# Down-projections of the second block with 7 block products in place of 8 for 1024 of 2816 features

## The reference

```python
def swiglu_2(h, w_gate, w_up, w_down):
    return (jax.nn.silu(h @ w_gate) * (h @ w_up)) @ w_down
...
        x = x + 0.5 * swiglu_2(rms_norm_2(x, ffn1_norm[l]), ffn1_w_gate[l], ffn1_w_up[l], ffn1_w_down[l])
```

## Time and profile before

| | |
|---|---|
| median of 3 runs | 1736.2 us |
| profiled execution | 1736.38 us, of which span 1734.6 us |
| TensorE busy | 1726.9 us (100%), 10296 matmuls |
| VectorE busy | 1230.0 us (71%) |
| ScalarE busy | 989.6 us (57%) |
| GpSimd busy | 111.4 us (6%) |
| HBM read | 312.10 MB, 181 GB/s over the span |

### The profile page before, as it was taken

How to read it: one execution, slowest core, us unless ns; L and a number is a source line. 1 busy time by engine, 2 the same in 40 slices (tenths; PEclk the granted TensorE clock), 3 DMA queues, 4 the chain that set the end, 5 groups by cost and what they waited for, 6 DMA issues and landing times.

```text
span 1734.6 us, 25928 instructions
## 1 busy us (share of the span) xinstructions
PE 1726.9 (100%) x10296; PEld 1487.0 (86%) x10296; DVE 1230.0 (71%) x1904; ACT 989.6 (57%) x1591; POOL 111.4 (6%) x196
## 2 busy tenths in 40 slices
PE   9999999999999999999999999999999999999999
PEld 7888888888888888888888888888888888888887
DVE  5877765668886777467756887775587648878762
ACT  6766554645555755365545666554565447666551
POOL 2100000702210000000001010000000001000000
PEclk9999999999999999999999999999999999999999
DMA  8545564654343555545454345555355534336551
GB/s 328 190 160 209 188 219 165 226 177 163 146 159 125 191 189 218 192 165 189 184 210 148 124 146 200 196 189 217 145 204 188 216 126 175 143 145 219 193 219 73
DMA packets 45561, 314.82 MB, mean 181 GB/s; under 512 B 5072, under 2 KB 5584, under 8 KB 8448
## 3 DMA queue, kind: packets, MB, share of 16 engines
q1 hardware_dynamic: 45056, 312.54, 49.2%
q10 hardware_dynamic: 288, 0.52, 0.1%
q0 software_dynamic: 96, 0.10, 0.0%
HBM read 312.10 MB, written 1.05 MB: 181 GB/s over the span
## 4 chain that ended last, share of the span: by engine, by line
PE 95%; DVE 1%; ACT 1%; DMA 1%; issue 1%; POOL 0%; SPq 0%; POOLq 0%; DVEq 0%; ACTq 0%
PE P L451 93%; DMA raw<-w_all 1%; PE P L464 1%; PE P L767 1%; DVE wl L1867 1%; ACT wh L1298 1%; PE P L668 0%; ACT nV L1338 0%; PE P L1202 0%; ACT xx L1333 0%; ACT wh L1311 0%; PE P L473 0%; PE P L1121 0%; PE P L1067 0%; DVE fce L2350 0%
## 5 line engine op out<-in xcount | busy, mean ns | idle before, releaser
L1867 DVE TENSOR_TENSOR wl<-raw,wh 128x2048 fp32r<-128x2048 f32 x287 | 656.5, 2294 | 184.5 <-ACT wh L1298 161.8
L1298 ACT ACTIVATE wh<-raw 128x2048 fp32r<-128x2048 f32 (+1 forms) x290 | 550.2, 1901 | 192.0 <-PE P L451 172.3
L451 PE MATMUL P<-xx,wh 128*128 128x512 f32 (+2 forms) x2800 | 643.1, 384 | 0.0
L451 PEld LDWEIGHTS P<-xx,wh 128*128 128x128 f32 (+1 forms) x2800 | 505.4, 188 | 96.7
L451 PE MATMUL P<-xx,wl 128*128 128x256 f32 x2688 | 350.8, 284 | 0.1
L451 PEld LDWEIGHTS P<-xx,wl 128*128 128x128 f32 x2688 | 340.3, 191 | 10.7 <-issue 0.3
L1434 ACT ACTIVATE ft<-P 128x256 f32<-128x256 f32 x240 | 90.1, 382 | 231.5 <-PE P L451 231.5
L451 PE MATMUL P<-wh,fhh 128*128 128x512 f32 x528 | 206.2, 390 | 0.0
L451 PE MATMUL P<-wh,fhl 128*128 128x512 f32 x528 | 205.5, 389 | 0.0
L451 PE MATMUL P<-wl,fhh 128*128 128x512 f32 x528 | 205.5, 389 | 0.0
L2030 DVE TENSOR_TENSOR fg<-P,ft 128x256 f32<-128x256 f32 x240 | 101.7, 424 | 121.9 <-ACT ft L1434 116.6
(11 more groups left out here) (340 smaller groups left out, 1458.7 us busy)
## 6 DMA issues: line engine op xcount, KB each, us to landing
raw<-w_all SPq DMA_DIRECT2D x289, 1024.0 KB, 4.8
nB<-rpb SPq DMA_DIRECT2D x4, 512.0 KB, 7.6
raw<-w_all SPq DMA_DIRECT2D x2, 512.0 KB, 7.0
xs<-x_in SPq DMA_DIRECT2D x1, 1024.0 KB, 9.4
fgb<-post SPq DMA_DIRECT2D x2, 512.0 KB, 5.6
out<-xs SPq DMA_DIRECT2D x4, 256.0 KB, 2.0
C<-cst SPq DMA_DIRECT2D x1, 770.5 KB, 8.7
ntm<-x_in ACTq DMA_DIRECT2D x2, 256.0 KB, 5.2
```

The costliest lines, as they stand in the source:

```text
L451: return t_.on.matmul(o, l, r, start=start, stop=stop, skip_group_check=True)
L1298: a.on.activation(o, i, ACT.Copy).then_inc(*hi.up((m,)))
L1867: v.on.tensor_tensor(o, i, h.bitcast(F32), ALU.subtract).then_inc(*lo.up(m))
```

## The change

In stages 4, 6, 7 and 9, eight of the 22 feature blocks are taken in pairs ("couples" (4,5), (6,7), (8,9), (10,11)). For such a pair, two tiles of tokens and two halves of outputs form a 2x2 by 2x2 product of blocks, done by seven block products and sums of blocks (Winograd's form of Strassen's scheme) in place of eight block products. Each block product is still three matmuls. The down pieces are ordered P S P S P S P S P P P: D1, D3, D5, D7 are the S pieces, each with both halves of one pair (21 matmuls); the other fourteen feature blocks are in the seven P pieces (24 matmuls).

- In the gate/up phase VectorE forms four sums of hidden features per pair (`couple_sums`), ScalarE rounds them (`couple_high`), VectorE takes the rest (`couple_low`).
- In the down-projection VectorE forms four sums T of weight blocks from the raw tile of each S piece (`sums_first`, at p = 0, 2, 4, 6), ScalarE rounds them (`sums_high`), VectorE takes the rest (`sums_low`). They lie in `xx`, one set for all four pairs, so that a set waits for TensorE's end with the one before. High and low parts of an S piece itself have 1536 columns.
- SP overwrites the raw tile of an S piece only when T has been formed from it (`"read"`).
- Products M1, M5, M6, M7 gather in banks 0, 1, 6, 7 over all four pairs, the others in banks 2, 3, 4 (bank 5 has no pair product). At p = 8 VectorE puts them together and into the residual (`sevens_end`), and adds the first half there, which was done at p = 5.
- The first turns of the next stage stand in D9 in place of D6.

Some buffers are laid out anew over existing memory, and the host packs the S pieces. The core of the diff:

```diff
+SEVEN = "PSPSPSPSPPP"
+COUPLES = [(4, 5), (6, 7), (8, 9), (10, 11)]
+SUMS_AT = {0: 0, 2: 1, 4: 2, 6: 3}
+SUMS_IN = (0, 0, 0, 0)
+SINGLE = [k for k in range(NF) if all(k not in c for c in COUPLES)]
+ALONE = [(k, h) for h in range(2) for k in SINGLE]
+LASTS = max(p for p in range(11) if SEVEN[p] == "S")
+MBANK = {"M1": 0, "M5": 1, "M6": 6, "M7": 7}
...
+    def sevens(name, layer):
+        left, couples = list(ALONE), list(COUPLES)
+        for kind in SEVEN:
+            if kind == "P":
+                out.append(("H", name, layer, tuple(left[:4])))
+                del left[:4]
+            else:
+                out.append(("S", name, layer, couples.pop(0)[0]))
...
+        SUM = tuple((h_[:, 0, :], h_[:, 1, :], f_[:, 1, :]) for h_, f_ in ((x2, xf2), (AF["fT"], AF["fTf"])))
+        SEVENS = [BASE[s_] + NF + p for s_ in (4, 6, 7, 9) for p in range(11) if SEVEN[p] == "S"]
...
+        def before_sums(s, u):
+            back = [w for w in range(u) if SUMS_IN[w] == SUMS_IN[u]]
+            if back:
+                return [mm.of("sum", s, back[-1])]
+            return [af.of("hh", s, NF - 1)] if SUMS_IN[u] else [mm.of("piece", BASE[s] + NF - 1)]
...
                     q.wait_ge(*lo.of(m - RAW))
+                    if m - RAW in SEVENS:
+                        q.wait_ge(*ls.of("read", m - RAW))
...
+                cbank = {(0, 0): 2, (1, 0): 3, (0, 1): 4, (1, 1): 5}
...
+                def three(b, ah_, al_, bh, bl, ready, end):
+                    if b not in begun:
+                        claim(b)
+                    t_.wait_ge(*ready[0])
+                    mul(P[b][:, :], ah_, bh, b not in begun, False)
+                    t_.wait_ge(*ready[1])
+                    mul(P[b][:, :], ah_, bl, False, False)
+                    t_.wait_ge(*ready[2])
+                    begun.add(b)
+                    return mul(P[b][:, :], al_, bh, False, end)
...
+                    B21, B11, B22 = (slice(a, a + 512) for a in (0, 512, 1024))
+                    T1, T3, T2, T4 = (slice(a, a + 512) for a in (0, 512, 1024, 1536))
...
+                    of_x(MBANK["M1"], k, 0, wh[n][:, B11], wl[n][:, B11], lo.of(m + p), whole)
+                    e = of_x(2, k + 1, 0, wh[n][:, B21], wl[n][:, B21], lo.of(m + p), ends[0, 0] == p)
+                    if ends[0, 0] == p:
+                        e.then_inc(*mm.up(("half", s, 0, 0)))
+                    of_s(4, 3, wh[n][:, B22], wl[n][:, B22], lo.of(m + p), False).then_inc(*mm.up(("piece", m + p)))
+                    t_.wait_ge(*hs.of("T", s, u, 0))
+                    of_s(MBANK["M5"], 0, th_[:, T1], tl_[:, T1], ls.of("T", s, u, 0), whole)
+                    of_s(MBANK["M7"], 1, th_[:, T3], tl_[:, T3], ls.of("T", s, u, 0), whole)
+                    t_.wait_ge(*hs.of("T", s, u, 1))
+                    of_s(MBANK["M6"], 2, th_[:, T2], tl_[:, T2], ls.of("T", s, u, 1), whole)
+                    e = of_x(3, k + 1, 1, th_[:, T4], tl_[:, T4], ls.of("T", s, u, 1), ends[1, 0] == p)
+                    e.then_inc(*mm.up(("sum", s, u), *([("half", s, 0, 1)] if ends[1, 0] == p else [])))
...
+                def after_seven(p, i, t):
+                    if s < 9:
+                        if p == 9 and i == 1:
                             turn(s + 1, 0, 0)
                             turn(s + 1, 1, 0)
-                        if t == 1 and i == 41:
+                        if t == 1 and p == 10 and i == 1:
                             turn(s + 1, 0, 1)
...
+                if m in SEVENS:
+                    w = 1536
...
+                def couple_high(u):
+                    a.wait_ge(*ls.of("S0", s, u))
+                    a.on.activation(flat(AF["fS"][:, u, 0, :, :]), flat(AF["fSf"][:, u, 1, :, :]),
+                                    ACT.Copy).then_inc(*hs.up(("S", s, u)))
+                def sums_high(u):
+                    h_, l_, f_ = sums(u)
+                    for z in range(2):
+                        n = slice(z * 1024, z * 1024 + 1024)
+                        a.wait_ge(*ls.of("T0", s, u, z))
+                        a.on.activation(h_[:, n], f_[:, n], ACT.Copy).then_inc(*hs.up(("T", s, u, z)))
...
+                    if s not in POST and p in SUMS_AT:
+                        sums_high(SUMS_AT[p])
+                    if s not in POST and p == 9 and s < 9:
...
+                def couple_sums(u):
+                    k = COUPLES[u][0]
+                    A1, A2 = fh[:, k % 3, :], fh[:, (k + 1) % 3, :]
+                    S1, S3, S2, S4 = (AF["fSf"][:, u, 1, i, :] for i in range(4))
+                    v.wait_ge(*vf.of("h", s, k + 1))
+                    v.on.tensor_tensor(S1, A1[:, toks(1)], A2[:, toks(1)], ALU.add).then_inc(*ls.up(("S1", s, u)))
+                    v.on.tensor_tensor(S3, A1[:, toks(1)], A1[:, toks(0)], ALU.subtract).then_inc(*ls.up(("S3", s, u)))
+                    v.wait_ge(*ls.of("S1", s, u))
+                    v.on.tensor_tensor(S2, S1, A1[:, toks(0)], ALU.subtract).then_inc(*ls.up(("S2", s, u)))
+                    v.wait_ge(*ls.of("S2", s, u))
+                    v.on.tensor_tensor(S4, A2[:, toks(0)], S2, ALU.subtract).then_inc(*ls.up(("S0", s, u)))
...
+                def couple_low(u):
+                    h_, l_ = (flat(AF["fS"][:, u, i, :, :]) for i in range(2))
+                    v.wait_ge(*hs.of("S", s, u))
+                    v.on.tensor_tensor(l_, flat(AF["fSf"][:, u, 1, :, :]), h_.bitcast(F32), ALU.subtract).then_inc(*ls.up(("S", s, u)))
...
+                def sums_first(u):
+                    n = m + NF + [p for p in range(11) if SEVEN[p] == "S"][u]
+                    h_, l_, f_ = sums(u)
+                    r_ = raw[n % RAW]
+                    v.wait_ge(*hi.of(n))
+                    for signal_ in before_sums(s, u):
+                        v.wait_ge(*signal_)
+                    v.on.tensor_tensor(grp(f_[:, 0:1024], 2), r_[:, 1536:2048].unsqueeze(1).broadcast_to([128, 2, 512]),
+                                       grp(r_[:, 512:1536], 2), ALU.subtract).then_inc(*ls.up(("T0", s, u, 0)))
+                    v.wait_ge(*ls.of("T0", s, u, 0))
+                    v.on.tensor_tensor(f_[:, 1024:1536], r_[:, 512:1024], f_[:, 512:1024],
+                                       ALU.subtract).then_inc(*ls.up(("T2", s, u)))
+                    v.wait_ge(*ls.of("T2", s, u))
+                    v.on.tensor_tensor(f_[:, 1536:2048], r_[:, 0:512], f_[:, 1024:1536],
+                                       ALU.subtract).then_inc(*ls.up(("T0", s, u, 1), ("read", n)))
+                def sums_low(u):
+                    h_, l_, f_ = sums(u)
+                    for z in range(2):
+                        n = slice(z * 1024, z * 1024 + 1024)
+                        v.wait_ge(*hs.of("T", s, u, z))
+                        v.on.tensor_tensor(l_[:, n], f_[:, n], h_[:, n].bitcast(F32),
+                                           ALU.subtract).then_inc(*ls.up(("T", s, u, z)))
+                def gather(t, hf, src):
+                    return v.on.scalar_tensor_tensor(xs[:, t, halfs(hf)], src, rh_[:, t:t + 1], xs[:, t, halfs(hf)], ALU.mult, ALU.add)
+                def sevens_end():
+                    banks = (2, 3, 4, 5)
+                    M1, M5, M6, M7 = (P[MBANK[n]][:, :] for n in ("M1", "M5", "M6", "M7"))
+                    U2, U3 = AF["ftm"][:, 0, 0:512], AF["ftm"][:, 0, 512:1024]
+                    M1s = AF["ftm"][:, 1, 0:512]
+                    v.wait_ge(*gx.of("rh", s))
+                    v.wait_ge(*mm.of("sum", s, len(COUPLES) - 1))
+                    v.on.tensor_copy(M1s, M1).then_inc(*ls.up(("M1", s)))
+                    v.wait_ge(*ls.of("M1", s))
+                    v.on.tensor_tensor(U2, M6, M1s, ALU.add).then_inc(*ls.up(("M6", s)))
+                    v.wait_ge(*ls.of("M6", s))
+                    v.on.tensor_tensor(U3, M7, U2, ALU.add).then_inc(*ls.up(("M7", s)))
+                    gather(0, 0, M1s).then_inc(*ls.up(("x00", s)))
+                    v.wait_ge(*ls.of("M7", s))
+                    gather(1, 0, U3).then_inc(*ls.up(("x10", s)))
+                    v.wait_ge(*ls.of("x00", s))
+                    add(s, 0, 0, banks, 0.5)
+                    v.wait_ge(*ls.of("x10", s))
+                    add(s, 0, 1, banks, 0.5)
+                    gather(1, 1, U3).then_inc(*ls.up(("x11a", s)))
+                    v.on.tensor_tensor(U2, M5, U2, ALU.add).then_inc(*ls.up(("U4", s)))
+                    v.wait_ge(*ls.of("x11a", s))
+                    gather(1, 1, M5).then_inc(*ls.up(("x11", s), ("M5", s)))
+                    v.wait_ge(*ls.of("U4", s))
+                    gather(0, 1, U2).then_inc(*ls.up(("x01", s)))
+                    v.wait_ge(*ls.of("x01", s))
...
                 rest(NF - 1)
                 banks = (2, 3, 4, 5)
                 for p in range(11):
+                    if s not in POST and p in SUMS_AT:
+                        sums_first(SUMS_AT[p])
+                    if s not in POST and p == LASTS + 1:
+                        sevens_end()
```

(40 more changed lines are left out.)

55 lines of the change are left out of this document (53 added, 2 removed).

## The result

| | median | range | against before, 95% interval |
|---|---|---|---|
| before | 1736.14 us | 1735.94 to 1736.23 | |
| after | 1761.61 us | 1761.05 to 1762.16 | 1.0144 [1.0132, 1.0156] |

The change makes the kernel 25.5 us slower; the forecast was 1760.7 us, 24.5 slower. One execution of the kernel before, run beside the last experiment, took 7890.72 us and is left out of all comparisons. From the profile page of the changed kernel, the lines that answer to the earlier trace rows: busy time by engine, and the lines of the chain that ended last.

The account below looks back on a forecast made before the run. TensorE, busy for all but 8 us, was taken to bound the kernel. Stages 6 and 7 at +6.5 us each, stage 4 at +6.9 and stage 9 at +4.5 were summed to +24.5 on 1736.2: 1760.7 us, range 1748 to 1772.

Parts of the forecast that it names:

- The signs: Down-projections: high parts idle for DMA, T sums 11.7 to 11.9 us apart, four TensorE waits a stage of 1.5 to 2.2.
- One sign of being wrong: Listed against the forecast: T sums 10.2 us apart, TensorE waits in the gate/up phase, or a granted clock below 1.00.
- The gain: TensorE in the four down-projections: 48 matmuls removed at 0.2267 us, 10.9 us, all on the path.
- The pair sums at nothing: Gate/up phase: sums of hidden features, 1.7 us a pair on VectorE, hidden beside TensorE and costed at nothing.
- The cover of 2.6 us a pair: Gate/up phase: VectorE's spare time beside TensorE, 1.3 us a piece, claimed to hide the pair sums.
- The ramp: Start of each down-projection: T's first low part stands at 9.74 us, TensorE wants it at 7.71 and waits 2.0.
- the added 0.36: Stage 4: VectorE leaves the gate/up phase 0.36 us later than in stage 6, lengthening the first wait.
- The turn: Down-projection loop from one T through fetch, high and low part to the next T: 11.75 us against TensorE's 10.20.
- the landing: Time for D4's fetch into D1's raw tile to arrive, within the loop between two T: 4.8 us.
- The fetch: Weight fetch of 1024 KB: 4.4 us by the skill page, median 4.8 in the trace; the page's total 6 us smaller.
- The tail: End of stages 4, 6, 7: TensorE waits 2.0 us for the addition before the third turn of `xs`; none in 9.
- The clock rival: TensorE: about 19 new gaps each drop the clock to 1.2 GHz for 11 matmuls, 47 us, some 1808; chance 0.03.

Follow-up runs that it names:

- the last experiment: Changed kernel with the fetches of D4, D6, D8, D10 and of the piece right behind each cut to half their bytes: 1746.78 us.
- opened through the tile: Changed kernel with D4, D6, D8, D10 fetched into memory free in the down-projection, computing instructions and order unchanged (also called the four tiles aside): 1737.02 us.
- opened through the order: Changed kernel with the low parts of D4, D6, D8 moved on VectorE behind the next T (also called VectorE's order alone): 1745.78 us.
- T's low part first: Changed kernel with T's low part made ahead of the other piece's low part in VectorE's order: 1760.44 us.
- the kernel that has no gap in the four stages: Changed kernel with VectorE's order rewritten and, on ScalarE, T's roundings ahead of the next high part; nothing left out: 1725.80 us.

## Why the prediction was right

- **The signs.** ScalarE's high parts of D4, D6, D8 and D10 do idle for the DMA, the T sums stand 11.5 to 11.9 us apart, and the third turn waits in stages 4, 6 and 7 and not in 9. Of the four waits a stage on T's low part, 13 of 16 came: in stages 6, 7 and 9 the second is missing (below). One sign of being wrong came too, a mean granted clock below 1.00 (0.997).
- **The gain**, 48 matmuls at 0.2267 us, 10.9: measured alone 10.7.
- **The pair sums at nothing**: confirmed by leaving them out. Each small addition was under-priced. From the groups by form of after, stages 5 and 6:

```profile
L2194 DVE TENSOR_TENSOR fSf<-fh,fSf 128x128 f32<-128x128 f32 x4 | 1.2, 293 | 0.1
L2208 DVE TENSOR_TENSOR xf<-raw 128x1024 f32<-128x1024 f32 x4 | 4.9, 1218 | 0.0
```

  0.29 us and not half of 0.42, since half the columns don't halve the operation. The cover of 2.6 us a pair was wide enough. The broadcast form of T, priced from rows of other operations at 1.22, came to 1.218; the 1536-column part, priced at 1.75 from a line between two sizes, to 1.75.
- **The ramp**: M5's second matmul went 9.96 us behind D0's start, not 9.74, because VectorE came out at 4.43 and not 4.2. I had dated D0 from its end, back over 24 matmuls; the first start lay 0.25 us earlier. The wait is 2.2 us, not 2.0. In stage 4 VectorE came out at the same 4.4, and the added 0.36 was not there.
- **The turn**: 11.5 to 11.9 us against 11.75, the landing 4.6 to 5.0. The second matmul of M5 went 9.96, 21.68, 33.18 and 45.47 us behind D0's start in stage 4. The prediction's times for it, without the 0.36 that it added for this stage, are 9.74, 21.49, 33.24 and 45.53. Four experiments move the turn and the time goes with it: opened through the tile (1737.0), opened through the order (1745.8), shortened by 0.3 and 0.9 us (1755.5, 1746.8). Two that leave it alone, though they take away a wait or a cost next to it, move little (1760.4, 1760.6).
- **The fetch.** The chain has landings of 4.6 to 5.0 us, with a second fetch behind, and halving both brought the landing to 3.85. The Trainium skill, "DMA: Bandwidth & Descriptors", Anatomy of one DMA, gives by its formula for the software path an estimated 4.4 us for 1024 KB and 3.2 for 512 KB. Both are below what this case's trace has on SP's queue, and with 4.4 the forecast would have been 6 us lower.
- **The tail**: TensorE's third turn started 1.65, 1.74 and 1.90 us late against 2.0, and moving one low part removed it.
- **The sum of the lag**: 35.0 us against 35.2 forecast (four times 7.2, the tails and stage 4's 0.36). That it is this close is in part luck. VectorE's exit was dated 0.23 us too early in four stages (+0.9 us), the turn 0.07 too long fifteen times (-1.0) and stage 4's 0.36 didn't come. The forecast's four stages also add up to 24.4 us, not 24.5.
- **The clock rival**, at 0.03, was half right, and "the rows at hand show no fall" was too weak a ground. One of the two rows was misread. The 2.75 us of idleness at the start lie ahead of TensorE's first instruction, and the first matmuls ran slow. TensorE's timeline of the kernel before:

```profile
2.75 2.08 PE L451 MATMUL P<-C 128*128 128x128 f32 x8 [2.75 <-DMA C<-cst]
4.61 1.06 PE L464 MATMUL P<-C,ntm 128*128 128x128 f32 x4
5.47 2.13 PE L451 MATMUL P<-C 128*128 128x128 f32 x12
...
13.02 1.03 PE L464 MATMUL P<-C,ntm 128*128 128x128 f32 x8
13.81 1.17 PE L451 MATMUL P<-wl,xx 128*128 128x512 f32 x4
```

  The four of L464 at 4.61 us take 0.86 us up to the next group, 0.21 each; the eight at 13.02 take 0.79, 0.10 each. So the start ran at about half speed. The trace's record of the granted clock begins only at 6.8 us, and the 1.00 of that window is of what follows. In the changed kernel the granted clock did fall behind the first gap in stages 6, 7 and 9 of the profiled execution, and not in stage 4. Windows behind that gap in stage 4 and in stage 6:

```profile
876.80:880.20 3.40, 3.31 (x15) 2.74 (x16) 1.17 (x2) 1.27 (x1) 0.00 (x0) 1.00 1.01 417
1193.40:1196.80 3.40, 3.37 (x9) 2.69 (x10) 1.11 (x1) 1.36 (x1) 0.00 (x0) 0.60 0.99 417
```

  And TensorE's timeline, the first eight matmuls there:

```profile
876.89 2.11 PE L495 MATMUL P<-xx,fS 128*128 128x512 f32 x8 [2.09 <-DVE xx L2222]
...
1193.43 3.27 PE L495 MATMUL P<-xx,fS 128*128 128x512 f32 x8 [2.06 <-DVE xx L2222]
```

  Behind gaps of 2.09 and 2.06 us the one stretch ran at a granted clock of 1.00 and the other at 0.60, a mean of the 2.4 and the 1.2 GHz level. The slow stretch cost about 1.6 us of TensorE, not the 2.5 that the rival reckoned with, but it lay within a turn that TensorE wasn't setting: in stage 6 the second wait (1.39 us in stage 4) is simply missing, and so it is in stages 7 and 9. Stages 4 and 6 grew by 6.33 and 6.44 us. The 47 us that I gave the rival would have needed a fall behind every gap, and no turn to absorb it.

What stays open is the last microsecond (after is 25.5 us over before by the medians, 24.3 by the four stages), and why the clock fell behind one gap and not behind a like one.

## What to carry to other kernels

An added reader of a buffer joins all that the buffer's release starts. Follow the release through fetch, landing and every queue that has the arriving data's work ahead of yours; if the path comes back to the reader, its length is a floor on the period, however idle the engines on it are. In such a closed path what lies beside it costs nothing (the single set, the slow stretches), gains come back at the exit (T's low part first), and what helps is to open it: another tile, or an order in which no engine's queue has the late tile ahead of the urgent work, on all engines at once.

## What the runs showed of the hardware

- A fetch of 512 KB with one of 1024 KB issued right behind landed in 4.47 us (4.2 to 4.6 in all the chain's turns), with one of 512 KB behind in 3.85 (3.6 to 4.0); 1024 KB with 1024 KB behind took 4.76 (4.6 to 5.0). The landing of a fetch depends on the one behind it.
- The granted clock fell behind a 2.2 us gap in some executions and stages and not in others. The kernel with the four tiles aside, in which nothing absorbs it, shows the price over its ten executions: 1734.7 us at a mean granted clock of 1.000 (one), 1736.2 to 1737.1 at 0.999 (five), 1737.6 to 1738.8 at 0.998 (four), so an estimated 1.7 us a fall. In the kernel that has no gap in the four stages the clock was 1.000 in all five, and the time within 1.4 us.
- Behind each gap of the four down-projections, of 0.24 us or of 2.3, the matmul after the late one started another 0.11 us late (run with VectorE's order alone).
- The first matmuls of the program, up to 6.7 us, ran at about half the speed of those behind.
